# A ring of four gathered rows and four chunk buffers in the tail of a decoder step

## What is computed

```
u    = peer_u[eid]                               # (tokens, 128, 2048)
act  = gelu(einsum('tkd,td->tk', u, xt))
coef = gate * act
y    = einsum('tk,tkd->td', coef, peer_v[eid])   # rows of peer_v, weighted and summed
```

## Time and profile before

| | |
|---|---|
| median of three runs | 4402.11 us |
| the profiled execution | 4408.91 us, its span 4406.9 us |
| TensorE busy | 3401.8 us (77%) |
| VectorE busy | 2648.8 us (60%) |
| GpSimd busy | 1446.1 us (33%) |
| DMA, whole span | 1316 MB, mean 299 GB/s |
| DMA from 2600 us on | 648 MB, mean 359 GB/s |

### The profile page before, as it was taken

The page is one execution under the profiler, slowest core; times in us unless marked ns, Lnnn a source line. Parts: engine busy times, 40 slices in busy tenths (PEclk is TensorE's granted clock), DMA queues, the critical chain, the costliest instruction groups (busy, mean ns, idle before and its releaser), DMA issues. The chain is left out here.

```text
span 4406.9 us, 33325 instructions
## 1 busy us (share of the span) xinstructions
PE 3401.8 (77%) x12703; PEld 2285.6 (52%) x12703; DVE 2648.8 (60%) x3886; ACT 673.2 (15%) x1696; POOL 1446.1 (33%) x868
## 2 busy tenths in 40 slices
PE   7979998969668888878887692111699996699990
PEld 6868887856543333566665471111544445544440
DVE  2350001848974444655657579999665549966668
ACT  2420000002222221000000100222600007500010
POOL 0000000025514444444546401888232212322236
PEclk9989999989888888989998896555599995599995
DMA  5334444459958777899989831999599998999999
GB/s 165 122 105 153 153 153 131 148 194 386 356 191 335 328 321 321 320 355 361 360 312 392 322 119 69 393 409 411 215 421 424 423 378 311 327 423 423 423 423 372
DMA packets 367761, 1316.36 MB, mean 299 GB/s; under 512 B 19525, under 2 KB 237286, under 8 KB 238578
## 3 DMA queue, kind: packets, MB, share of 16 engines
q0 software_dynamic: 124416, 939.58, 52.9%
q1 hardware_dynamic: 242398, 374.30, 24.0%
q10 hardware_dynamic: 788, 0.36, 0.0%
HBM read 1307.33 MB, written 6.83 MB: 298 GB/s over the span
## 5 line engine op out<-in xcount | busy, mean ns | idle before, releaser
L227 POOL DMA_INDIRECT area<-in_peer_u_dram,area x544 | 936.2, 1721 | 2220.1 <-DVE area L238 981.1
L238 DVE CUSTOM_DVE_ANT_0 area<-area 128x2048 f32<-128x2048 f32 x544 | 1231.0, 2287 | 252.4 <-DMA area<-in_peer_u_dram,area 250.6
L1651 PE MATMUL PS<-area 128*128 128x512 f32 x2048 | 879.3, 592 | 0.0
L244 DVE SCALAR_TENSOR_TENSOR area<-area 128x2048 f32<-128x2048 f32 x288 | 676.8, 2350 | 203.3 <-DMA area<-in_peer_v_dram,area 179.6
L227 POOL DMA_INDIRECT area<-in_peer_v_dram,area x288 | 462.5, 1606 | 649.4 <-DVE area L244 548.0
L1651 PEld LDWEIGHTS PS<-area 128*128 128x128 f32 x2048 | 389.1, 190 | 489.8 <-issue 489.8
L1637 PE MATMUL PS<-area 128*128 128x64 f32 x1024 | 251.2, 427 | 394.3 <-issue 245.6
L1129 PE MATMUL PS<-area 128*128 128x256 f32 (+1 forms) x2048 | 485.5, 400 | 37.0 <-DMA area<-in_w_in_dram 32.0
L1129 PEld LDWEIGHTS PS<-area 128*128 128x128 f32 x2048 | 396.9, 194 | 123.9 <-DMA area<-in_w_in_dram 33.8
L1637 PEld LDWEIGHTS PS<-area 128*128 128x128 f32 x1024 | 228.2, 328 | 418.5 <-issue 293.4
L1214 PE MATMUL PS<-area 128*128 128x256 f32 (+1 forms) x1280 | 283.5, 384 | 31.4 <-DMA area<-in_w_out_dram 28.0
(11 more groups left out here) (249 smaller groups left out, 2515.3 us busy)
## 6 DMA issues: line engine op xcount, KB each, us to landing
area<-in_peer_v_dram SPq DMA_DIRECT2D x128, 1024.0 KB, 9.0
area<-in_w_in_dram SPq DMA_DIRECT2D x56, 2048.0 KB, 8.2
area<-in_w_out_dram SPq DMA_DIRECT2D x16, 2048.0 KB, 8.6
area<-in_peer_wq_dram SPq DMA_DIRECT2D x16, 2048.0 KB, 8.7
area<-in_w_att_up_dram SPq DMA_DIRECT2D x16, 1024.0 KB, 5.7
area<-in_w_lru_up_dram SPq DMA_DIRECT2D x16, 1024.0 KB, 8.7
area<-in_peer_u_dram,area POOLq DMA_INDIRECT x544, 10.1
area<-in_x_prompt_dram SPq DMA_DIRECT2D x8, 1024.0 KB, 7.2
```

Of the source, the lines that this page charges most:

```text
L227: g_.indirect_dma_start(ring[SLOT[c]], None, io[("peer_u", "peer_v")[table]][0], bass.IndirectOffsetOnAxis(ap=slot_col(eid0, eid1, tb, j), ...
L238: v.tensor_tensor_reduce(row, row, Xn[(0, 1, 0, 1, 0)[tb]], 1.0, 0.0, ALU.mult, ALU.add, act).then_inc(s_used, 1)
L244: v.scalar_tensor_tensor(dst, row, act, dst, ALU.mult, ALU.add).then_inc(s_used, 1)
L1651: ins = pe.matmul(PS[:, 4 * b + q, :], spread[i // 32][:, i % 32, P * b:P * (b + 1)], vrows[n % 3][:, 512 * q:512 * (q + 1)], start=False, ...
```

## The change

`RING2` becomes 4. The slot that the ring gives up becomes a fourth buffer for chunks of peer_v. SP issues chunk 3 together with chunk 2, and from then on chunk n when chunk n-4 has been used. The amount of data, the number of instructions on DVE, TensorE, ACT and POOL and their order stay as they are.

```diff
-RING, RING2 = 6, 5
+RING, RING2 = 6, 4
...
-        vrows = [at(o, D) for o in (45472, 47520, RING2 * D)]
+        vrows = [at(o, D) for o in (45472, 47520, RING2 * D, (RING2 + 1) * D)]
...
-        s_vin = [sem(f"v_chunk{n}_in") for n in range(3)]
+        s_vin = [sem(f"v_chunk{n}_in") for n in range(4)]
...
-                        sp_.dma_start(vrows[n % 3], io["peer_v"][0][NK * n:NK * (n + 1), :]).then_inc(s_vin[n % 3], 16)
+                        sp_.dma_start(vrows[n % 4], io["peer_v"][0][NK * n:NK * (n + 1), :]).then_inc(s_vin[n % 4], 16)
...
                     chunk(2)
+                    chunk(3)
...
-                    for n in range(3, NK):
-                        sp_.wait_ge(s_chunk, n - 2)
+                    for n in range(4, NK):
+                        sp_.wait_ge(s_chunk, n - 3)
                         chunk(n)
...
-                            pe.wait_ge(s_vin[n % 3], 16 * (n // 3 + 1))
+                            pe.wait_ge(s_vin[n % 4], 16 * (n // 4 + 1))
...
-                                                    vrows[n % 3][:, 512 * q:512 * (q + 1)], start=False, stop=i == NH1 - 1)
+                                                    vrows[n % 4][:, 512 * q:512 * (q + 1)], start=False, stop=i == NH1 - 1)
```

## The result

The changed kernel takes 4444.91 us (median of four runs, 4435.0 to 4450.68) against 4403.84 us (four runs, 4401.68 to 4409.27) for the kernel before: ratio 1.0093, 95% interval 1.0075 to 1.0110. That is +41 us where +22 was forecast, and outside the range. The profiled execution took 4450.01 us, its span 4448.2 us, 41.3 us more than the span of before.

The account below looks back on a forecast made before the run. The tail was taken as bound by gathers and DVE's columns, with TensorE never waiting for chunks. Terms 12.6 + 1 + 2.5 + 5.7 = 21.8 us on 4402.11 gave 4423.9, predicted as 4424 us; range 4407 to 4440.

Parts of the forecast that it names:

- The sign: Whole kernel: slower than before, given a chance of 0.78.
- the slow lap: Reuse of one slot when POOL waits out a column: 10.8 us, or 2.70 us a column with four slots.
- the first term of the sum: The remaining 24 batches, 258.7 us in place of 246.1: +12.6 us, bounds 0 or a gain, and +17.4.
- The fourth chunk buffer: Chunk loads for the products: removes no wait, since TensorE never waits for a chunk; 0 us.
- The second products: Columns beside the second products: rate stays at 3.86 us a column and 424 GB/s; 0 us.
- the queue argument: Second products: gather time is a queue behind full engines, so one row less shortens it 3.9 us, rate unchanged.
- Rival 2: Second products become bound by the ring, each lap of four 1 us longer: 25 us more, 4449 us; chance 0.12.
- +1 + 2.5 + 5.7 = 9.2: +1 at 3838 to 3860 us, +2.5 for 20 columns at 4276 to 4328 us, +5.7 for the last 24.
- The batches at 10.78 us with four slots: The pace of before's eight batches from 2746.05 to 2832.31 us holds for the remaining 24.
- POOL's late instruction as the reason: Batches: POOL's instruction begins under a column and ends 0.7 to 0.8 us after it, so four slots are in play.
- Rivals 1 and 3: 1: not slower, POOL starts in DVE's gaps, 4400 or 4387 us, 0.10; 3: nothing binds, 4402 us, 0.10.
- The gain of rival 1: Batches at 9.9 us from the first on give back 15 us: 4387 us; half of that rival's 0.10.

Follow-up runs that it names:

- e1: Kernel before with four slots from column 352 on, but still three chunk buffers: 4446.06 us, 1.0104 of before.
- e4: The whole change repeated, measured beside its parts on the same chip: 4447.77 us, 1.0100 of before.
- e9: Kernel before with three slots from column 352 to the end, three chunk buffers: 4561.70 us, 1.0367 of before.
- e3: Kernel before with five slots for columns 352 to 479, four from 480 on, three chunk buffers: 4418.29 us, 1.0036 of before.
- e10: Eight slots for columns 352 to 479, then the change's four slots and four chunk buffers: 4407.53 us, 1.0014 of before.
- e6: Kernel before with eight slots for columns 352 to 479, five later, three chunk buffers: 4394.02 us, 0.9977 of before.
- e2: Kernel before with four slots for columns 352 to 479 only, five later, three chunk buffers: 4431.55 us, 1.0083 of before.
- e11: As e2, but block 2's indices replaced so that POOL gathers neighbouring rows: 4442.99 us, 1.0122 of before.
- e7: As e2, but SP loads neighbouring rows in place of POOL's gathers for columns 352 to 479: 4395.39 us, 0.9980 of before.
- e8: As e7, SP loading columns 352 to 479, but with five slots throughout: 4395.25 us, 0.9982 of before.

## Why the prediction was wrong

The sign, the place and the mechanism of the slow lap held. The step that failed is the first term of the sum, +12.6 us for the batches: it measured +27.7.

- *The fourth chunk buffer, 0.* Right as far as the runs can tell (e1 beside e4: 1.7 us, with some 10 us of play; TensorE's 0.0 us of waits on both sides).
- *The second products, and the queue argument.* Right: 3.9 us a column, 423 GB/s, landing 3.9 us earlier. Rival 2 would have needed one slot less (e9: 4.02 us a column).
- *What comes after the start of the first products, +1 + 2.5 + 5.7 = 9.2.* The profile has +9.9, but by luck: the three terms were each off. From the start of the products to the 20 columns before the norms (which begin at 4275.92 us before and at 4307.0 after) the change loses nothing (-0.4), those 20 columns take 58.6 us in place of 52.0 (+6.6, outside the bounds of 2.0 to 4.5), and the last 24 lose 3.7 and not 5.7. Over many runs the sum is more: e3 has +18.0, e10 13.6 over e6. In the profiles of e1, e3, e4 and e10 the 20 columns lose 5.2 to 10.0 us; that term was too small. DVE's waits in them run up to 3.3 us in the change's profile, so an undisturbed lap was the wrong price here too.
- *The batches at 10.78 us with four slots.* This is the term that failed: forecast +12.6, measured +27.7 in the profile and +31.3 in e2. The lap was right. The undisturbed intervals of the change are 10.7 us. What the sum set against them was wrong. Before's mean of 10.26 us contains waits for gathers (9.93 us is its undisturbed interval; 7.6 us of waits in all over 23 intervals), and the 10.78 was read from eight intervals that happened to contain no long one. I compared a mean with an undisturbed value: 10.69 against 9.93 us over 23 intervals is already +17.5. And the disturbances don't stay as they are when the slot that absorbed them goes: 18.2 us in the change's profile against 7.6 in before's, another +10.7. With -0.7 from the first eight intervals this is the +27.5. e4, e2, e1 and e11 show the same, 8 to 13 intervals over 11.4 us.
- *POOL's late instruction as the reason.* Supported, not isolated: without POOL four slots cost nothing (e7), with POOL and the same kind of rows everything (e11), and the first, slow batches of before go when POOL can start early (e6). The lock of the Trainium skill, page "SBUF — State Buffer", section "SBUF: two separate sides", by which GpSimd can't write a DMA's descriptors while DVE holds the pair of ports that they share, would give this; no run took the lock away and left POOL's gathers.
- *Rivals 1 and 3* (not slower, nothing binds): excluded by the intervals of the batches and the result. The gain of rival 1, batches at 9.9 us or less from the first, exists, but it takes eight slots (e6) or loads by SP (e7, e8).

What stays open is what makes single gathers land after 9.5 to 10.8 us, where 7.7 is the median, while the DMA engines carry less than before. The SP loads of e7 don't show it (8.3 at most; e8's land after up to 12.9 us, but at 422 GB/s and with five slots full). Nor do the three slots of e9, which POOL gathers into (8.3 at most). A burst of gathers that POOL writes behind each other after a catch-up is in the example above, but it was not isolated.

The version to keep is e6: eight slots in the batches, five later, three chunk buffers, 0.9977 of before (0.9966 to 0.9988), and some 50 us below the change.

## What to carry to other kernels

Before a slot is taken from a ring, count from issue to reuse how many are really in play, at each stretch; where the issuing engine runs late, that number is the ring's real depth, and the last slot is what absorbs late landings. When a steady pace is read from a few clean periods, set it against the clean periods of the other side, and price the disturbances apart: they grow when the reserve goes. And a buffer is worth something only to a consumer that waits: TensorE had 0.0 us of waits for chunks, so a fourth could bring nothing.

## What was not expected of the hardware

Four slots loaded from SP's queue keep the DMA engines at 418 GB/s with a DMA share of 1.01 (e7). Four slots gathered from POOL's queue carry 360 to 383 GB/s over the same 300 us (e11, e4, the change, e1, e2), and the DMA share is still 0.95 to 0.99: a high busy share doesn't say that the engines run at full rate. Eight slots bring POOL's gathers to 422 GB/s (e6). The packets themselves take longer. Queue, packets, MB and share of the 16 engines from 2750 to 3050 us, in the change and in e7:

```profile
q0 software_dynamic: 15237, 110.99, 96.4%
q1 hardware_dynamic: 17227, 125.44, 101.1%
```

Share times 16 engines times 300 us, by packets, gives 0.304 us a packet in the change, 0.282 in e7. In the traces most 8 KB packets take 0.31 us, but some take more than 0.5: 6.3% of them in the change, 5.4% in e2, 2.4% before, 0.4% in e7, 0.3% in e6, and 9.1% in e9. They are most frequent where the fewest loads are in play; why is open.
